# Modulation weights of an adaptive-norm block: eight column groups interleaved over the partitions of one accumulator, two in another, and their sums at the seams

## The reference

```python
c_act = jax.nn.silu(c)                                       # 1 x 2048
mod = (c_act @ w_ada[l] + b_ada[l])[:, None, :]              # w_ada: 2048 x 12288
sh1, sc1, g1, sh2, sc2, g2 = jnp.split(mod, 6, axis=-1)
h = rms_norm(x, norm_mix[l]) * (1.0 + sc1) + sh1
x = x + g1 * hybrid_mixer(h, ...)
h = rms_norm(x, norm_ffn[l]) * (1.0 + sc2) + sh2
x = x + g2 * conv_glu_ffn(h, ...)
```

## Time and profile before

| | |
|---|---|
| median of 3 runs | 2351.09 us (2350.31 to 2352.11) |
| the profiled execution | 2352.51 us, of it the span 2350.7 us |
| busy, share of the span | TensorE 99%, VectorE 69%, ScalarE 49%, GpSimd 0% |
| TensorE matmuls | 17937 |
| granted TensorE clock, mean over the span | 0.997 |
| moved over the transfer queues | 543.62 MB, 231 GB/s on average |

### The profile page before, as it was taken

How to read it: one execution, slowest core, us unless ns; L and a number is a source line. 1 busy time by engine, 2 the same in 40 slices (tenths; PEclk the granted TensorE clock), 3 DMA queues, 4 the chain that set the end, 5 groups by cost and what they waited for, 6 DMA issues and landing times.

```text
span 2350.7 us, 43754 instructions
## 1 busy us (share of the span) xinstructions
PE 2337.8 (99%) x17937; PEld 2151.6 (92%) x17937; DVE 1616.4 (69%) x1931; ACT 1153.2 (49%) x1510; POOL 5.1 (0%) x7
## 2 busy tenths in 40 slices
PE   9999999999999999999999999999999999999998
PEld 8889778999999999888999899888999999998887
DVE  5668568777777766877778455667878666665556
ACT  5565454534344344444764444546544445454444
POOL 0000000000000000000000000000000000000000
PEclk9999999999999999999999999999999999999999
DMA  8556567888888877898577545555778656665563
GB/s 308 167 179 197 159 234 271 278 282 297 282 282 295 282 242 263 316 324 315 175 279 269 163 130 153 196 200 187 283 255 295 208 179 206 196 206 197 192 192 117
DMA packets 233049, 543.62 MB, mean 231 GB/s; under 512 B 15610, under 2 KB 22596, under 8 KB 232260
## 3 DMA queue, kind: packets, MB, share of 16 engines
q1 hardware_dynamic: 232756, 540.97, 68.3%
q10 hardware_dynamic: 144, 0.52, 0.1%
HBM read 535.11 MB, written 6.32 MB: 230 GB/s over the span
## 4 chain that ended last, share of the span: by engine, by line
PE 98%; DVE 0%; ACT 0%; issue 0%; DMA 0%; SPq 0%; DVEq 0%; ACTq 0%
PE ps L330 37%; PE ps L1858 18%; PE ps L608 18%; PE ps L2216 16%; PE ps L1875 2%; PE ps L2509 0%; PE ps L1041 0%; PE ps L1053 0%; PE ps L1071 0%; PE ps L1083 0%; PE ps L2141 0%; PE ps L460 0%; PE ps L2744 0%; PE ps L1134 0%; PE ps L2921 0%
## 5 line engine op out<-in xcount | busy, mean ns | idle before, releaser
L297 DVE TENSOR_TENSOR weights_lo<-raw_weights,weights_hi 128x1024 fp32r<-128x1024 f32 x786 | 957.6, 1224 | 659.8 <-ACT weights_hi L289 658.0
L289 ACT ACTIVATE weights_hi<-raw_weights 128x1024 fp32r<-128x1024 f32 x782 | 827.2, 1062 | 1086.8 <-PE ps L330 446.4
L516 DVE SCALAR_TENSOR_TENSOR ada_acc<-ada_w,col,ada_acc 128x1024 f32<-128x1024 f32 x180 | 230.2, 1279 | 0.1
L330 PE MATMUL ps<-conv_x_hi,weights_hi 128*128 128x256 f32 x1280 | 198.0, 277 | 0.0
L330 PE MATMUL ps<-glu_x_hi,weights_hi 128*128 128x256 f32 x1280 | 197.7, 276 | 0.0
L330 PE MATMUL ps<-glu_x_hi,weights_lo 128*128 128x256 f32 x1280 | 197.2, 276 | 0.0
L330 PE MATMUL ps<-glu_x_lo,weights_hi 128*128 128x256 f32 x1280 | 197.2, 276 | 0.0
L330 PE MATMUL ps<-conv_x_lo,weights_hi 128*128 128x256 f32 x1280 | 197.2, 276 | 0.0
L330 PE MATMUL ps<-conv_x_hi,weights_lo 128*128 128x256 f32 x1280 | 197.2, 276 | 0.0
L330 PEld LDWEIGHTS ps<-conv_x_hi,weights_hi 128*128 128x128 f32 x1280 | 169.1, 188 | 1.0 <-issue 1.0
L330 PEld LDWEIGHTS ps<-glu_x_hi,weights_hi 128*128 128x128 f32 x1280 | 169.0, 188 | 0.0
(11 more groups left out here) (560 smaller groups left out, 3635.3 us busy)
## 6 DMA issues: line engine op xcount, KB each, us to landing
raw_weights<-in_w_in_dram SPq DMA_DIRECT2D x202, 512.0 KB, 5.0
ada_w<-in_w_ada_dram SPq DMA_DIRECT2D x96, 1024.0 KB, 6.1
raw_weights<-in_w_ffn_up_dram SPq DMA_DIRECT2D x176, 512.0 KB, 4.6
raw_weights<-in_w_gate_dram SPq DMA_DIRECT2D x88, 512.0 KB, 4.6
raw_weights<-in_w_up_dram SPq DMA_DIRECT2D x88, 512.0 KB, 4.6
raw_weights<-in_w_down_dram SPq DMA_DIRECT2D x88, 512.0 KB, 5.7
raw_weights<-in_w_ffn_down_dram SPq DMA_DIRECT2D x88, 512.0 KB, 4.3
raw_weights<-in_w_out_dram SPq DMA_DIRECT2D x64, 512.0 KB, 5.1
```

Source lines behind the costliest of these rows:

```text
L289: kit.nc.scalar.activation(kit.slots(n, i)[0], raw, ACT.Copy).then_inc(kit.w_hi, 1)
L297: kit.nc.vector.tensor_tensor(lo, raw, hi.bitcast(F32), ALU.subtract).then_inc(kit.w_lo, 1)
L330: ins = nc.tensor.matmul(out, lhsT=lhsT, rhs=rhs, start=start and m == 0, stop=(k == KT - 1 and m == 2), skip_group_check=True)
L516: step = nc.vector.scalar_tensor_tensor(acc, w, c, acc, ALU.mult, ALU.add)
```

## The change

The accumulation is turned round. Groups 0 to 7 are no longer made one after the other: a step now takes 16 rows of `w_ada` across all eight groups (8192 columns), and puts row r, group g on partition 8r + g. One step's tile is 128x1024 as before, there are 128 steps as before, and they all add into one accumulator; partition p of it holds a partial sum of group p mod 8. Groups 8 and 9 share a second accumulator in the same way, 64 rows by two groups a step. The scalar on each partition has to follow: `c_oct` holds each element of `silu(c)` eight times and `c_half` twice; they come from two small row tiles widened by two VectorE copies, through one more turned pack. In the gate/up loop the 16 columns of a turn are first copied to `glu_c`.

The eight groups are summed once, at the seam to `Mixer2`, by eight products with a mask of 128x8 (`oct`), and VectorE adds the bias in the same operation (`Ada.summed`); the two groups at the seam to `ConvGlu`, with a mask of 128x2 (`half`). The transposes (`turn_sums`) and the reductions (`reduce_sums`) are gone. The accumulator of group 8 isn't stored alone any more: group 9's products go on from it, and one tile is stored and brought back. Each step has a transfer of its own, 512 KB in place of 1 MB, with the rows as the outermost dimension, and four semaphores take turns where two did. The load of `final_w` moves behind the first product of the down stage. Among the mixers' other waits only the numbers of reused semaphores change.

```diff
-def turn_sums(kit, acc, bank):
-    for q in range(8):
-        step = kit.nc.tensor.transpose(kit.ps[:, bank + q // 4, (q % 4) * P:(q % 4 + 1) * P], acc[:, q * P:(q + 1) * P],
-                                       kit.c("ident"))
-    return step
-def reduce_sums(kit, a, bank):
-    return kit.nc.vector.tensor_reduce(kit.modcols[:, ds(a, 8)], kit.ps[:, bank:bank + 2, :].rearrange(
-        "p b (q n) -> p (b q) n", n=P), AX, ALU.add)
...
+    def source(self, lead, j, s):
+        w = self.kit.ins["w_ada_2"][0]
+        if lead < 8:
+            rows = w[ds(OCT * (16 * lead + s) + 16 * OCT * j, OCT), 0:16 * UN]
+        elif lead < 10:
+            rows = w[HALF * (16 * (lead - 8) + s):HALF * (16 * (lead - 8) + s + 1), 16 * UN:20 * UN]
+        else:
+            rows = w[P * s:P * (s + 1), 2 * UN * lead:2 * UN * (lead + 1)]
+        return rows.rearrange("r (g n) -> r g n", n=2 * UN)
...
+        kit, a = self.kit, 8 * lead + m
         if a >= 2:
             sp.wait_ge(kit.ada_acc, 2 * (a - 1) + 16 * j)
-        w = kit.ins["w_ada_2"][0]
-        sp.dma_start(self.w[:, m % 2, :, :], w[2 * m * P:2 * (m + 1) * P, ds(2 * UN * lead + 2 * UN * j, 2 * UN)]
-                     .rearrange("(k p) n -> p k n", p=P)).then_inc(kit.ada_w[m % 2], 16)
-    def product(self, dve, lead, j, s, acc=None):
+        for s in (2 * m, 2 * m + 1):
+            sp.dma_start(self.w[:, m % 2, s % 2, :], self.source(lead, j, s)).then_inc(kit.ada_w[s % 4], 16)
+    def scalar(self, lead, s):
+        name, first = ("c_oct", 0) if lead < 8 else ("c_half", 8) if lead < 10 else ("c_2", lead)
+        return self.kit.cols(name, 16 * (lead - first) + s)
+    def product(self, dve, lead, j, s, acc=None, prior=None, c=None):
...
         acc = self.acc if acc is None else acc
-        if k == 0:
-            dve.wait_ge(kit.ada_w[m % 2], 64 * lead + 64 * j + 16 * (m // 2 + 1))
-        w, c = self.w[:, m % 2, k, :], kit.cols("c_2", s)
-        if s:
+        dve.wait_ge(kit.ada_w[s % 4], 64 * lead + 64 * j + 16 * (s // 4 + 1))
+        w, c = self.w[:, m % 2, k, :], self.scalar(lead, s) if c is None else c
+        if s == 0 and lead in (0, 8, 10, 11):
+            step = nc.vector.tensor_scalar(acc, w, c, None, ALU.mult)
+        else:
             dve.wait_ge(kit.ada_acc, 16 * lead + s + 16 * j)
-            step = nc.vector.scalar_tensor_tensor(acc, w, c, acc, ALU.mult, ALU.add)
-        else:
-            step = nc.vector.tensor_scalar(acc, w, c, None, ALU.mult)
+            step = nc.vector.scalar_tensor_tensor(acc, w, c, acc if prior is None else prior, ALU.mult, ALU.add)
         step.then_inc(kit.ada_acc, 1)
...
+    def sums(self, pe, bank, mask, acc):
+        kit, (a, b) = self.kit, self.kit.at[mask]
+        n = b - a
         for q in range(8):
-            step = nc.tensor.matmul(kit.ps[:, bank, q:q + 1], lhsT=self.acc[:, q * P:(q + 1) * P],
-                                    rhs=kit.c("ones")[:, 0:1], start=True, stop=True)
+            step = kit.nc.tensor.matmul(kit.ps[:, bank, n * q:n * (q + 1)], lhsT=acc[:, q * P:(q + 1) * P],
+                                        rhs=kit.c(mask), start=True, stop=True)
         step.then_inc(kit.ada_sum, 1)
...
+    def summed(self, lead, bank, mask):
+        kit, (a, b) = self.kit, self.kit.at[mask]
+        n, first, bias = b - a, 8 * lead, COLS["b_ada_2"] + 8 * lead
+        cols, add = (x.rearrange("p (g q) -> p q g", q=8) for x in (kit.modcols[:, first:first + 8 * n],
+                                                                    kit.col[:, bias:bias + 8 * n]))
+        return kit.nc.vector.tensor_tensor(cols, kit.ps[:, bank, 0:8 * n].rearrange("p (q g) -> p q g", g=n), add, ALU.add)
...
+        last = n == len(self.packs) - 1
+        if n >= len(self.packs) - 2:
+            pe.wait_ge(self.s_cwide, 2)
+        rows = self.pack[0:w, 0 if last else n, :]
+        kit.nc.tensor.transpose(kit.ps[:, 6, 0:w], rows, kit.c("ident")[0:w, 0:w]).then_inc(self.s_packT, 1)
...
+        if n == self.PACK + len(self.packs):
+            pe.wait_ge(self.s_col, len(self.packs))
...
+        if n == self.PACK + len(self.packs):
+            act.wait_ge(self.s_col, len(self.packs))
+            for a, b in ((COLS["c_half"], COLS["b_ada_2"]), (COLS["c_oct"], NCOLS)):
+                step = nc.scalar.activation(kit.col[:, a:b], kit.col[:, a:b], ACT.Silu)
+            step.then_inc(self.s_csilu, 1)
...
+        if n == len(self.packs) - 4:
+            dve.wait_ge(self.s_packs, 16 * sum(len(p[0]) for p in self.packs[1:]))
+            _, to, _, _, _ = self.packs[-2][0][0]
+            self.kit.nc.vector.tensor_copy(self.pack[:, 0, :].rearrange("p (r g) -> p r g", r=OCT),
+                                           self.c_rows[:, :].unsqueeze(2).broadcast_to([P, OCT, P // OCT])
+                                           ).then_inc(self.s_cwide, 1)
+            self.kit.nc.vector.tensor_copy(self.pack[0:to, len(self.packs) - 2, :].rearrange("p (r g) -> p r g", r=HALF),
+                                           self.c_rows_2[0:to, :].unsqueeze(2).broadcast_to([to, HALF, P // HALF])
+                                           ).then_inc(self.s_cwide, 1)
...
                             pe.wait_ge(mixer.s_g2lo, 12)
-                            mid()
                         mixer.turn_glu(pe, n)
                 return
-            multiply_block(kit, pe, x, "T", 0, first, i, uses[0], mid)
+            multiply_block(kit, pe, x, "T", 0, first, i, uses[0])
...
-                if summed and s == begun:
-                    self.ada.reduced(dve, self.lead, j)
                 if half is not None and s % 2 == begun:
-                    self.ada.product(dve, self.lead, j, 8 * half + s // 2)
+                    q = 8 * half + s // 2
+                    if q == 0:
+                        a = COLS["c_oct"] + 16 * self.lead
+                        dve.wait_ge(kit.ada_acc, 16 * self.lead + 16 * j)
+                        nc.vector.tensor_copy(self.c_turn[:, :], kit.col[:, ds(a + 16 * j, 16)]).then_inc(self.s_c, 1)
+                        dve.wait_ge(self.s_c, 1 + j)
+                    self.ada.product(dve, self.lead, j, q, c=self.c_turn[:, q:q + 1])
...
-                    self.ada.product(dve, self.lead + s // 16, 0, s % 16, self.accs[s // 16])
+                    self.ada.product(dve, self.lead + s // 16, 0, s % 16, self.accs[s // 32], None if s else self.ada.acc)
...
+    def ada_sums(self, pe):
+        pe.wait_ge(self.kit.ada_acc, 128)
+        self.ada.sums(pe, 0, "oct", self.accs[0])
+    def ada_summed(self, dve):
+        dve.wait_ge(self.kit.ada_sum, 1)
+        self.ada.summed(0, 0, "oct").then_inc(self.kit.ada_out, 1)
+        dve.wait_ge(self.kit.ada_out, 1)
...
         pe.wait_ge(self.squares_in, 8)
-        self.down.ada_sums(pe, 0)
-        self.down.ada_sums(pe, 1, 0, 2)
+        self.down.ada_sums(pe)
         pe.wait_ge(self.squares_in, 11)
         for k in range(4):
             self.turned.turn_early(pe, k)
-        self.down.ada_sums(pe, 1, 2, 8)
         for k in range(4):
             self.turned.turn(pe, k)
...
+        self.down.ada_summed(dve)
         modulation(kit, 0)
...
-            self.ada.product(dve, self.lead, 0, self.ADA.index(n))
+            s = self.ADA.index(n)
+            self.ada.product(dve, self.lead, 0, s, prior=None if s else self.down.accs[1])
...
     def scale_sums(self, pe):
-        kit, mixer = self.kit, self.mixer
-        pe.wait_ge(mixer.s_accs, 16)
-        pe.wait_ge(kit.pair_free[0], self.uses[0] + 1)
-        for q in range(8):
-            step = kit.nc.tensor.matmul(kit.ps[:, 1, q:q + 1], lhsT=mixer.accs[:, 0, q * P:(q + 1) * P],
-                                        rhs=kit.c("ones")[:, 0:1], start=True, stop=True)
-        step.then_inc(kit.ada_sum, 1)
-        pe.wait_ge(mixer.s_xlast, ST)
-        turn_sums(kit, mixer.accs[:, 1, :], 2).then_inc(kit.ada_sum, 1)
-    def first_scales(self, dve):
-        kit, a = self.kit, 4 * KT
-        b = COLS["b_ada_2"] + a
-        dve.wait_ge(kit.ada_sum, self.lead - 1)
-        kit.nc.vector.tensor_tensor(kit.modcols[:, a:a + 8], kit.ps[:, 1, 0:8], kit.col[:, b:b + 8], ALU.add
-                                    ).then_inc(kit.ada_out, 1)
-    def last_scales(self, dve):
-        kit, a = self.kit, 4 * KT + 8
-        dve.wait_ge(kit.ada_sum, self.lead)
-        reduce_sums(kit, a, 2).then_inc(kit.ada_out, 1)
-        dve.wait_ge(kit.ada_out, self.lead)
-        kit.nc.vector.memset(kit.stat[:, 59:60], 0.0).then_inc(kit.pair_free[1], 1)
-        add_bias(kit, a, 8)
-        modulation(kit, 1, 8, KT)
-        kit.nc.vector.memset(kit.stat[:, 58:59], 0.0).then_inc(self.s_scales, 1)
+        pe.wait_ge(self.mixer.s_accs, 16)
+        pe.wait_ge(self.kit.pair_free[0], self.uses[0] + 1)
+        self.ada.sums(pe, 1, "half", self.mixer.acc_back)
+    def scales(self, dve):
+        dve.wait_ge(self.kit.ada_sum, 2)
+        self.kit.dve(self.ada.summed(8, 1, "half"))
...
```

(41 more changed lines are left out.)

127 lines of the change are left out of this document (42 added, 85 removed).

## The result

The changed kernel takes 2410.61 us (median; 2399.89 to 2418.53) against 2351.6 us in runs beside it: a ratio of 1.0248, 95% interval 1.0208 to 1.0289. It is 59 us slower where 6 us less were forecast, and far outside the range.

What follows compares the result with a forecast made beforehand. TensorE, busy 2337.8 of 2350.7 us, was taken as the bound. Terms -5.34 + 0.15 - 0.94 + 0.10 = -6.03 us gave 2346.5 us profiled, 2345.1 us as median (0.26% faster); range 2342.8 to 2348.8.

Steps and rivals of the forecast that it cites:

- slower: the new transfers: Modulation-weight transfers in the down stage: DMA engines become the bound, at 1.5 per byte 16 us, 2361 us; chance 0.05.
- Part 5: VectorE and the queues: multiply-adds, column copies and 192 instead of 96 transfers are covered; cost 0.
- Part 1: Transposes inside TensorE's stream: 48 transposes of `ada_acc` go, 0.89 us for each of six groups, 5.34 us saved.
- Part 2: The front: one more turned pack and a wider one cost +0.15 us; widening copies and Silus cost 0.
- Part 3: Seam at 1147 us: fewer narrow products, late transposes (L2141) start 0.94 us earlier; bounds 0.45 to 1.2.
- Part 4: Seam at 1612 us: the eight transposes were hidden, 0; VectorE's mean waits for the sum, +0.1 us; bounds 0 to 0.3.
- The clock: TensorE's granted clock at both seams: taken as before, falling to half at 1147 us and kept full at 1612 us.
- the rival that had 0.20: Seam at 1612 us: a second fall of TensorE's clock, price 2.0 us, giving 2347.1 us; chance 0.20.
- The sum: Whole kernel: the terms add to -6.03 us, profiled 2346.5 us, median 2345.1 us; chance of the forecast 0.52.

Runs made afterwards that it cites:

- before_split: The kernel before, with each 1 MB transfer of modulation weights cut in two of 512 KB, same rows and columns: 2351.57 us, ratio 0.9999.
- flat_block: The changed kernel, with each transfer of groups 0 to 7 reading one contiguous 512 KB block, 128 outermost: 2347.44 us, ratio 0.998.
- rows_by_eight: The changed kernel, groups 0 to 7 loaded from 128 separate 4 KB rows of one group, written as 16 blocks of 8: 2411.61 us, ratio 1.0278.
- spacing_alone: Transfers alone, to 8 partitions 1, 4, 8, 12 apart: median packets 0.619, 0.159, 0.328, 0.159 us; 16 partitions 1, 4, 8 apart: 0.618, 0.331, 0.328.
- plain_source: The changed kernel, with groups 0 to 7 loaded from the rows and columns the kernel before reads, 512 KB each: 2346.87 us, ratio 0.998.
- quads: The changed kernel with four column groups interleaved instead of eight (32 outermost), two accumulators, the second's sums in the first seam: 2348.78 us, ratio 0.9986.
- quads_fill: quads plus eight accumulator transposes that nobody reads, as filler in the second seam: 2346.9 us, ratio 0.9978 to the kernel before.

## Why the prediction was wrong

The step that failed is the one under the rival "slower: the new transfers", at "Against it: the runs that are written stay 4 KB, and the other transfers of half a megabyte run well beside them". Both facts hold, and neither bears on the matter. Size is harmless (`before_split`) and so is the form of the reads (`flat_block`); what counts is the source's outermost count (`rows_by_eight`), and by `spacing_alone`, though not shown in the change itself, which partitions the engines then write together. The prediction named the new form (16 rows, and 64 for the pairs, where 128 had stood) and judged it by bytes and run lengths alone; no row of the trace before shows what such a form costs. So it gave this 0.05.

- **The rival's mechanism was right, its size not.** It put the border in the down stage at a ratio of 1.28 per byte and guessed 1.5. In the down window the engines' time per byte rose from 0.90 / 323 to 1.03 / 280, by 1.32 over all; with 40% of the bytes in the new form that is 1.8 for these, the ratio of the packets alone (0.29 / 0.159); in the first gate/up window, from 0.85 / 299 to 1.02 / 256, it rose by 1.40, more than 1.8 would give there, as the other packets are slower too. It priced the down stage only. Gate/up has the same form at 35% of its bytes ((14.9 - 9.7) / 14.9 MB in its window of the earlier trace rows) and its border at about 1.5; at 1.8 it is over that too. Measured against the plain source: 32.3 us in gate/up and 30.1 in down, 62.4 of 63.5 us of span. TensorE's waits for `weights_lo` in the two loops are 39 us of it; the rest is about its sum of busy time, 24.4 larger than with the plain source (2353.9 against 2329.5) for as many matmuls, at the lower clock. How much of that the full queue would have taken anyway no run shows.
- **Part 5**, "at its cover this is 0": right for the issues, the copies and the first products (`plain_source`), wrong for the transfers themselves, which it counted by their issue alone.
- **Part 1**, forecast 0.89 a group: with the plain source the stretch between the same transposes of `x_rows` (428.64 before, 428.54 with the plain source) and the sums is 4.77 us shorter, for five groups 0.95 each. The forecast was 0.4 too small over six. The whole gate/up stage is 5.7 us shorter (480.2 instead of 485.9), forecast 5.3.
- **Part 2**, +0.15: from the first product of weights (7.12 us before, 7.39 with the plain source) to the first of gate/up (422.25, 423.03) it takes 0.51 us more, 0.36 above the forecast. It is not measured by itself, and `before_split` differs from the kernel before by 0.16 there.
- **Part 3**, forecast -0.94: from the sums to the late transposes 3.83 us with the plain source, 4.73 before: -0.90. The gap before the transposes is 1.48 us, forecast 1.5.
- **Part 4**, forecast +0.10: from the early transposes to the late 3.80 us instead of 3.66: +0.14; the idle time is 1.14 us, forecast 1.1.
- **The clock.** It was taken as before at both seams. It falls at the second seam as well, the rival that had 0.20. From the late transposes to the next it took 4.34 us before (1615.63 to 1619.97), in the change 6.41 (1671.46 to 1677.87), 2.1 more, where I had taken 2.0; with the plain source it is 0.8 more (0.50 from 1610 to 1612 us), in `quads` 1.5. At the first seam it falls, and with the plain source is low for 3.4 us instead of 6.8; that gives nothing back, the stretch takes 5.84 us instead of 5.80. `quads_fill` shows that the missing work was the cause of the second fall. The rule of the Trainium skill that idle stretches lose the clock (TensorE: Matmul & The Clock Gate, Part 1: The HAM clock gate) agrees, and should have made this rival the likelier one.
- **The sum** of -6.03 us stands beside -5.9 us of span and -4.7 us of medians for the plain source, whose 2346.87 is within the range. That the span agrees to 0.1 us is luck in part: the fall at the second seam (0.8) and most of the front's cost (0.4) were not in the sum, part 1 gave more than forecast, and the stretch between the seams, which no term touches, came out 0.8 us shorter (1158.12 to 1611.97 before, 1152.39 to 1605.42 with the plain source; in `quads` it was not shorter). The single terms were right to half a microsecond; the term that was left out, at 0 under part 5, was ten times their sum.

## What to carry to other kernels

When a transfer's layout changes, ask first what its outermost count is now, and which partitions the DMA engines may then write together; bytes, run lengths and partition count can all stay while the time per packet nearly doubles (0.159 to 0.29 us). A queue at 0.85 to 0.90 has a border near: work out the ratio for every stage that carries the new form, and if nothing in the trace excludes it, let the range reach there. A transfer's form can be measured alone in a few hundred microseconds before it is built in.

## What the runs showed of the hardware that was not expected

A DMA packet's time depends on where the transfer's partitions lie: 4 KB took 0.159, 0.33 or 0.62 us for the same reads, by how far apart they lay. Other traffic on the same engines suffers with it: the 2 KB packets of the weights' tiles went from a median of 0.084 to 0.127 us between 450 and 500 us, and a tile of `w_down` took 12.4 us to land instead of 5.7. With 32 or 64 outermost in the source a transfer to 128 partitions ran within 12% of plain rows (363 to 381 against 409 GB/s), with 16 at 60% (245). And eight transposes that nobody reads, in an idle gap of 1.14 us, saved 1.5 us by keeping TensorE's clock at 1.00.
